# A cached-attention step reordered: value products and sigmoids moved in six and four steps, a lag of three rows in paired groups, eight small scalings moved to ScalarE

## The reference, cut to what matters

```
# even layer, per HGRN2 head (4 heads, 128 wide)
f = lb + (1 - lb) * sigmoid(z);  k = (1 - lb) * sigmoid(-z);  q = silu(q_raw) * K ** -0.5
o, S = gated_linear_scan(q, k, v, log(f), s0)      # running sum of log f, decays, products
o = rmsnorm(o) * silu(g)
# even layer, cached attention of the samples: 8 sequences, 64 pages of 128 rows each
past = cache_mla[e][page_table]                     # 8192 rows of 320 numbers per sequence
p = softmax([q_lat, q_pe] . lat * scale);  out = p @ lat[..., :256]
```

## Time and profile before

| | |
|---|---|
| median of 3 runs | 3249.51 us |
| the profiled execution, its own time | 3246.02 us |
| its span | 3244.2 us |
| PE busy in the span | 3151.0 us (97%) |
| DVE, ACT, POOL busy | 1209.9 us, 1021.5 us, 787.1 us |
| mean granted clock of TensorE | 0.989 |

### The profile page before, as it was taken

One profiled execution on the slowest core, in us unless ns is written; L12 is line 12 of the kernel. 1 busy time (PEld: TensorE's weight loads), 2 busy tenths in 40 slices (PEclk: granted clock), 3 DMA queues, 4 the chain that ended last, 5 costly groups with the idle time before them and its releaser, 6 DMA issues. The chain is left out here.

```text
span 3244.2 us, 51079 instructions
## 1 busy us (share of the span) xinstructions
PE 3151.0 (97%) x21197; PEld 2934.1 (90%) x21197; DVE 1209.9 (37%) x2011; ACT 1021.5 (31%) x1657; POOL 787.1 (24%) x437
## 2 busy tenths in 40 slices
PE   7999999899999999999999999999999999999998
PEld 7998667677678999999999989998899999999998
DVE  4122365556543422222222326724434222222223
ACT  4111435555652311222211342312434211222212
POOL 1122104444531112222122114721121112222121
PEclk9999999999999999999999999999899999999999
DMA  5222205656653111111111134667431111111112
GB/s 192 74 81 70 72 20 194 221 179 242 208 206 101 39 46 46 45 40 44 45 45 45 46 110 141 224 224 283 149 108 46 40 46 45 45 45 39 45 45 75
DMA packets 235208, 325.61 MB, mean 100 GB/s; under 512 B 13120, under 2 KB 190208, under 8 KB 234800
## 3 DMA queue, kind: packets, MB, share of 16 engines
q1 hardware_dynamic: 215056, 234.80, 22.1%
q0 software_dynamic: 20000, 88.64, 7.9%
HBM read 255.98 MB, written 67.42 MB: 100 GB/s over the span
## 5 line engine op out<-in xcount | busy, mean ns | idle before, releaser
L103 PE MATMUL mlp_bank<-mlp_a_hi,mlp_w_hi 128*128 128x352 f32 (+1 forms) x1536 | 503.2, 328 | 0.9 <-DVE mlp_a_lo L567 0.9
L105 PE MATMUL mlp_bank<-mlp_a_hi,mlp_w_lo 128*128 128x352 f32 (+1 forms) x1536 | 503.1, 328 | 0.0
L104 PE MATMUL mlp_bank<-mlp_a_lo,mlp_w_hi 128*128 128x352 f32 (+1 forms) x1536 | 502.7, 327 | 0.0
L103 PE MATMUL mlp_bank<-mlp_x_hi,mlp_w_hi 128*128 128x384 f32 x1488 | 486.7, 327 | 2.9 <-POOL mlp_w_lo L539 2.9
L105 PE MATMUL mlp_bank<-mlp_x_hi,mlp_w_lo 128*128 128x384 f32 x1488 | 486.3, 327 | 0.0
L104 PE MATMUL mlp_bank<-mlp_x_lo,mlp_w_hi 128*128 128x384 f32 x1488 | 485.9, 327 | 0.0
L583 DVE TENSOR_TENSOR xT<-xT,mlp_bank 128x352 f32<-128x352 f32 (+1 forms) x384 | 202.7, 532 | 520.0 <-PE mlp_bank L105 520.0
L539 POOL TENSOR_TENSOR mlp_w_lo<-mlp_raw,mlp_w_hi 128x1024 fp32r<-128x1024 f32 x64 | 154.3, 2411 | 629.6 <-ACT mlp_w_hi L494 629.6
L575 DVE SCALAR_TENSOR_TENSOR mlp_relu<-mlp_bank,mlp_rstd 128x352 f32<-128x352 f32 (+1 forms) x192 | 102.5, 534 | 527.6 <-PE mlp_bank L105 508.8
L539 POOL TENSOR_TENSOR mlp_w_lo<-first,mlp_w_hi 128x1024 fp32r<-128x1024 f32 x62 | 148.9, 2402 | 605.9 <-ACT mlp_w_hi L494 605.9
L103 PEld LDWEIGHTS mlp_bank<-mlp_a_hi,mlp_w_hi 128*128 128x128 f32 x1536 | 288.6, 188 | 2.0 <-DVE mlp_a_lo L567 2.0
(11 more groups left out here) (518 smaller groups left out, 5681.8 us busy)
## 6 DMA issues: line engine op xcount, KB each, us to landing
first<-in_w_up SPq DMA_DIRECT2D x32, 512.0 KB, 4.2
mlp_raw<-in_w_up SPq DMA_DIRECT2D x32, 512.0 KB
first<-in_w_down SPq DMA_DIRECT2D x32, 512.0 KB
mlp_raw<-in_w_down SPq DMA_DIRECT2D x32, 512.0 KB
projections<-odd_zout SPq DMA_DIRECT2D x24, 544.0 KB, 4.2
forms<-gla_f SPq DMA_DIRECT2D x20, 544.0 KB, 2.7
residual<-xT SPq DMA_DIRECT2D x2, 4352.0 KB, 14.8
projections<-even_zout SPq DMA_DIRECT2D x16, 544.0 KB
```

The source lines that it names most:

```text
L103: pe.matmul(out, w_hi, x_hi, start=first, stop=False)
L104: pe.matmul(out, w_hi, x_lo, start=False, stop=False)
L105: return pe.matmul(out, w_lo, x_hi, start=False, stop=last)
```

## The change

It edits four places.

1. `first_two_groups`: group 1 follows three rows behind group 0. In `even_stage` the last sum of squares stands at step 7 instead of 8. The steps of the sums in the other stages stay as they are.
2. Mix stage, six steps (7, 8, 15, 16, 23, 24): PE takes value(step-1) behind all key blocks, not behind the first two. DVE's `gather(step - 1)` follows it to a place behind block 6's copy, which in the steps 7, 15 and 23 is between the clamp and the scan of `running_sum`.
3. Mix stage, ACT: `sigmoids` of the next head move from the slot ahead of `copy_p` to a place behind `copy_p` and block 0's copy (steps 5, 13, 21); in the steps 5, 13, 21 and 29 the blocks 4 and 5 are copied ahead of the exponentials.
4. `even_out_stage`: the new rows' probabilities `pn` (32 by 512) are multiplied by their shares in eight activations of 32 by 64 on ACT, not in one operation on DVE.

```diff
-    LAG = 2
-    SUMS_AT, LAST_SUM_AT = (3, 5) if norm.own is None else (7, 8)
+    LAG = 3
+    SUMS_AT, LAST_SUM_AT = (3, 5) if norm.own is None else (7, 7)
...
+    def value_late(step):
+        return step > 0 and any(2 * step + 1 + LEAD - SLOTS * h in (3, 5) for h in range(HEADS))
+    def sigmoids_at(step):
+        return any(2 * step + LEAD - SLOTS * h == 14 for h in range(HEADS))
...
-                if step:
+                if step and not value_late(step):
                     value(step - 1)
                 if later:
                     for u in range(2, UNITS):
                         turn_keys(step + 1, u)
+                if value_late(step):
+                    value(step - 1)
                 slot(2 * step + 1)
...
-                    if own_slot == -2 and h:
-                        sigmoids(h)
...
+            def after_copies(n):
+                for h in range(1, HEADS):
+                    if n + LEAD - SLOTS * h == -2:
+                        sigmoids(h)
...
                     copy_keys(step + 1, 0)
-                    copy_keys(step + 1, 2)
+                after_copies(2 * step)
+                early = (2, 4, 5) if sigmoids_at(step) else (2,)
+                if later:
+                    for u in early:
+                        copy_keys(step + 1, u)
                 exponentials(step)
...
+            def last_keys(step):
+                copy_keys(step + 1, 6)
+                gather(step - 1)
...
-                if step:
+                if step and not value_late(step):
                     gather(step - 1)
...
+                if value_late(step):
+                    slot(2 * step + 1, lambda: last_keys(step))
+                    if not has_running_sum(2 * step + 1):
+                        last_keys(step)
...
+            act.wait_ge(shared, 1)
+            for b in range(NB):
+                end = act.activation(M.pn[:, b, :], M.pn[:, b, :], ACT.Copy, scale=share_new[:, b:b + 1])
+            end.then_inc(pn_shared, 1)
-            dve.wait_ge(shared, 1)
-            dve.tensor_tensor(M.pn[:], M.pn[:], share_new[:].unsqueeze(2).broadcast_to([Q, NB, NS]), ALU.mult).then_inc(pn_shared, 1)
```

More of the change, by code:

```diff
@@ L1969, in _ @@
                     copy_keys(step + 1, 0)
-                    copy_keys(step + 1, 2)
+                after_copies(2 * step)
[3 more added lines that the diff above has]
+                        copy_keys(step + 1, u)
                 exponentials(step)
                 if later:
-                    for u in (4, 5, 7, 8, 9):
+                    for u in ACT_UNITS[1 + len(early):]:
                         copy_keys(step + 1, u)
@@ L2198, in _ @@
                     copy_keys(step + 1, 3)
-                slot(2 * step + 1, lambda: copy_keys(step + 1, 6))
-                if later and not has_running_sum(2 * step + 1):
-                    copy_keys(step + 1, 6)
+                if value_late(step):
+                    slot(2 * step + 1, lambda: last_keys(step))
+                    if not has_running_sum(2 * step + 1):
+                        last_keys(step)
+                else:
+                    slot(2 * step + 1)
+                    if later:
+                        copy_keys(step + 1, 6)
                 bank_slot(2 * step + 1)
```

## The result

| | kernel before | changed kernel |
|---|---|---|
| median | 3249.38 us (3249.14 to 3252.26, 4 runs) | 3270.48 us (3265.51 to 3271.42, 4 runs) |
| ratio, 95% interval | | 1.0062 [1.0046, 1.0078] |
| the profiled execution, its span | 3246.02, 3244.2 us | 3271.42, 3269.6 us |
| mean granted clock of TensorE | 0.989 | 0.979 |
| even stage | 278.23 us | 275.92 us |

The change makes the kernel 21.1 us slower (forecast: 8.6). The spans differ by 25.4 us: the profiled execution of the kernel before lay 3.4 us under its median, that of the changed one 0.9 us over its own. Stage and step lengths are differences between the first starts of stages or scores in the two traces.

What follows compares the result with a forecast made beforehand. PE has work for 97% of the span, so only its idle time can be won. Terms -10.3 + 21.6 - 2.0 - 0.7 = +8.6 us on a 3249.5 median gave 3258, range 3243 to 3271.

Steps and rivals of the forecast that it cites:

- rival A: The forecast itself: gathers starve PE in steps 16, 17 and their like; 3252 to 3266 us, chance 0.5.
- the landing of the last gather: Fourth gather (j = 3) of step 17's pages: taken to land at 760, within 758.7 to 760.8.
- the clock: Half-clock stretches of 1.6 us: -3.2 for those in steps 7 to 9 before, +3.2 for a third of six after.
- Sigmoids (edit 3): Steps 5, 13, 21: PE's waits ahead of value and last key blocks go, 3.0 us each; step 29 1.3; sum -10.3.
- Values late, up to block 0 of step 17: Value(14) ends 4.0 us late, delaying gathers; PE gets block 0 at 757, wanted at 749.6; score(17) +4.3 us.
- Rival D: Worse: SP's transfers meet the late gathers, landings take 9.5 us, TensorE stays at 1.2 GHz behind idles; 3275, chance 0.15.
- Step 17: Value(16) starts 2.9 us later after score(17), held by POOL's difference behind four gathers, two ACT activations and copy_p.
- Sum for edit 2: Late values in three triples of steps, 7.2 us each: +21.6 us with clock terms cancelling; bounds +6 and +39.
- Lag (edit 1): Even stage gains 0.7 and 1.6 us for a half-clock stretch; three other stages +0.1 each; sum -2.0, bounds -2.3, +4.
- Shares (edit 4): Output stage: eight activations take 1.2 to 1.5 us, PE goes on 1.3 earlier; -0.7 us, bounds 0 and -3.
- Rival B: Faster: step 17's pages come within 2 us of PE's asking, late values cost under 6 us; 3242, chance 0.15.

Runs made afterwards that it cites:

- scan_first: Changed kernel with DVE's running-sum scan ahead of gather(step - 1) in steps 7, 15, 23; 3264.22 us (one run).
- pool_order: Changed kernel with POOL's difference ahead of the fetch in the steps with a late value; 3262.83 us (one run).
- late_ring13: Changed kernel with a ring of 13 gathers instead of 12, so a fetch's first gather needs no late value; 3265.56 us (one run).
- values_back: Changed kernel with the value products and DVE's gather back in their old place, the other three edits kept; 3228.23 us, ratio 0.9965 to the kernel before.
- values_back_again: Same kernel as values_back, repeated on another chip; 3228.32 us, ratio 0.9973 to the kernel before.
- lag_shares: Kernel before with only the three-row lag and the shares in eight ACT activations, mix stage unchanged; 3236.26 us, ratio 0.9994.
- values_only: Kernel before with only the late value products added; 3272.96 us, ratio 1.01.
- ring13: Changed kernel with values in their old place and a ring of 13 gathers instead of 12; 3220.44 us, ratio 0.9946 to the kernel before.
- late_no_fetch: Changed kernel without the gathers that late values release, using older pages, so attention differs from the reference; 3236.13 us (one run).

## Why the prediction was right

It said slower with 0.58, 3258 in 3243 to 3271; the median is 3270.5. The mechanism was rival A's, and two of its terms, the landing of the last gather and the clock, were too small. That the range held is luck in part: the rise is 21.1 us where 8.6 was forecast, the median lies half a microsecond under the upper bound, two of the four runs lie above it, and (A) itself had 3252 to 3266.

- **Sigmoids (edit 3): right.** Forecast -3.0 in three steps and -1.3 in one; measured 18.54 to 15.53 three times, and 16.82 to 15.29: -10.6. ACT's timeline in step 13 shows the planned order, copy_p, block 0, three sigmoids, then three copies ahead of the table load:

```profile
712.95 0.60 ACT L1842 ACTIVATE mix_pT<-mix_KB 128x512 f32<-128x512 f32 x1 [1.04 <-PE mix_KB L1681]
...
716.92 1.57 ACT L1823 ACTIVATE mix_keys<-mix_KB 128x512 f32<-128x512 f32 x3
718.51 1.28 ACT L1830 ACT_TABLE_LOAD   x1
```

- **Values late, up to block 0 of step 17: right.** Value(14) was to end 10.2 us after score(15) and ended at 10.3. The second gather's issue was to end at +14.0, held by the scan, and ended at +14.1 with 2.22 us. Block 0 was forecast at +20.8 and came at +19.8. The SBUF — State Buffer page of the Trainium skill, under Who interferes with whom, infers that a DVE product with two inputs in SBUF leaves descriptor generation alone. The traces disagree: an issue beside the scan took 2.22 us, and in `scan_first` the issues that began while such a product ran took 1.59 and 1.49. The third issue of the changed kernel (755.61), which began just ahead of a product (755.64), took 0.95.
- **The landing of the last gather: mis-sized.** I took j = 3 at +23.8, 7.35 us behind its issue's end; block 5 started at +25.9. The window's rows give a landing of 9.6 in the median for these four gathers, beside three transfers of 544 KB. Rival D had named long landings beside SP's transfers; that these transfers are the cause is not shown. It cost 2.0 us in this triple.
- **Step 17: right but for the clock.** Forecast +2.9, measured 19.61 against 15.23, +4.4. Of that 1.65 is half clock, seen in two rows: blocks 0 and 1 took 1.59 instead of 1.04, value(16) 3.03 instead of 1.93. The cause that came last was not the one I named: I had value(16) behind POOL's difference and ACT's decays. PE waited 2.59 us for pages ahead of block 0, and `pool_order` took the difference away without a gain. The cause that I named stands right behind it: in `late_ring13` the pages are in time, and step 17 still loses 1.6 us to it.
- **Clock: too small.** I took a third of six stretches in the nine steps (+3.2) and no more. The nine steps of the changed kernel run 37.5 us at half clock (13.7 of them in step 8), those of before 6.8, though part of it lies in waits. Beyond them the steps 14, 22 and 30 each have a stretch of 3.4 us and no wait above 0.5 us: +1.65 three times. Such stretches also stand in kernels without late values (22 and 30 in `values_back`, 6, 14 and 30 in `values_back_again`, 14 and 22 in `lag_shares`), so these 5 us are not edit 2's; what places them stays open.
- **Sum for edit 2.** Forecast +21.6, the nine steps give +32.8: two of the triples lost 11.1 and 11.0, the one at step 15 10.6, where 7.2 was forecast, plus clock. The bounds of 6 and 39 held it. The second cost, DVE's chain behind the late gather, was missed altogether. It is hidden here; what would remain of it if the pages came at once is not measured, and is about 1 us a step by the estimate above.
- **Lag (edit 1): right in kind.** Even stage -2.3 (forecast -2.3, of which 1.6 for a half-clock stretch), the three other stages +0.1, +0.3, +0.2 (forecast +0.1 each). By `lag_shares` 0.7 of the 2.3 are there with the stretch still standing, as the sum had it. PE's wait changed its name from POOL's low weights to `mlp_x_lo`, as forecast. In the even stage PE stops for the last addition:

```profile
56.46 1.98 PE L296 MATMUL even_sum<-acc,ones 128*128 128x512 f32 x4 [2.00 <-DVE acc L325]
```

- **Shares (edit 4): the wait mis-sized.** It fell from 2.80 to 2.03 only, not to 1.5, since the eight activations took 2.00 us and not 1.2 to 1.5. The stage gained 2.3 (forecast 0.7, bounds 0 and 3): 0.8 of it is there in `lag_shares` too, and the other 1.5 is a half-clock stretch that is gone here and in three of the other eleven traces with this edit. PE's row:

```profile
1012.94 0.44 PE L3301 MATMUL evenout_B<-ident,mla_pn 32*64 32x32 f32 x8 [2.03 <-ACT mla_pn L3191]
```

- **Not in the sum:** the stage behind the odd one is 1.6 us longer with nothing edited in it (a half-clock stretch more; so it is in `values_only`, and not in `ring13`), the load 0.8.
- **Rival B** (pages in time) fell: in the steps 8, 16 and 24 they come 5.7 to 9.0 us after PE asks. The prediction's estimate of 3.5 us for a landing, worked out from the fit in DMA: Bandwidth & Descriptors of the Trainium skill, under Anatomy of one DMA, is half of the median of 7.3 that the trace shows.

## What to carry to other kernels

When a consumer is moved to a later place to fill an idle gap, look first at what its completion releases: here 2 us won ahead of score(16) were paid with 8 us in step 16 and 4 in step 17, because four gathers were waiting for each late product. A prefetch that hangs on a late release can be helped by one more slot in the ring for its first transfer: here -7.9 us, where the late values cost 34. And look behind the moved operation in every queue: the small addition that followed the value took DVE's scan along, and with it the copy on which PE depends.

## What the runs showed of the hardware that I had not expected

**The same rows of PE, two times.** In the kernel before, ACT's last two key copies of step 15 come late; in `values_back_again` they follow at once. ACT's timelines, the kernel before and then `values_back_again`:

```profile
744.28 1.77 ACT L1814 ACTIVATE mix_keys<-mix_KB 128x512 f32<-128x512 f32 x3
746.92 1.33 ACT L1814 ACTIVATE mix_keys<-mix_KB 128x512 f32<-128x512 f32 x2 [0.87 <-PE mix_KB L1653]
```

```profile
734.05 2.54 ACT L1821 ACTIVATE mix_keys<-mix_KB 128x512 f32<-128x512 f32 x5
```

PE's rows for these blocks stand at the same distances from score in both, so its modelled ends don't show that blocks 8 and 9 were really finished 1.3 to 1.5 us later. It goes with the chip: the kernels with early values in these steps have it where the kernel before takes 3249 to 3251 us and don't where it takes 3237 to 3239. It reaches the steps 3, 4, 11, 12, 19, 20 and 28 with 0.3 to 0.5 us (in one of six traces of those chips, `late_ring13`, it does not). The steps 0 to 31 took 452.67 us in the kernel before and 444.90 in `lag_shares`, which has the same mix stage; that is most of the 12 us between the chips' medians. What delays PE there stays open. A wait of PE of 2.24 us ahead of score(16) that I had put down to ACT was in part this.

**DVE and POOL slow each other.** DVE's product at the chunk ends (128 by 1024, and a small one behind it) took 1.36 us in the changed kernel, where POOL was issuing gathers, and 4.97 in `late_no_fetch`, where POOL's two differences ran beside it and took 5.89 us. Two differences took 3.97 us in `pool_order`, where DVE made no such product beside them.
